# Stick-breaking values in a decoder layer: high and low part of a head's values side by side as one stationary block of 128 columns, the two halves of the result summed afterwards

## The reference, cut to what matters

```
def one_block(args):                      # 128 queries against all keys
    z = einsum('bhqd,bhkd->bhqk', q_blk, kf)
    log_beta = log_sigmoid(z)
    log_rem = where(mask, log_sigmoid(-z), 0.0)
    later = cumsum(log_rem, axis=3, reverse=True) - log_rem
    w = where(mask, exp(log_beta + later), 0.0)
    return einsum('bhqk,bhkd->bhqd', w, vf)
```

## Time and profile before

| | us |
|---|---|
| median of 3 runs (2136.02 to 2138.6) | 2136.45 |
| the profiled execution | 2141.96 |
| its span in the profile | 2140.1 |
| PE busy in the span | 2021.9 |
| stick-breaking stage, 600 to 880 us of the span | 280.0 |
| PE busy in that stage | 263.73 |

### The profile page before, as it was taken

One profiled execution on the slowest core, in us unless ns is written; L12 is line 12 of the kernel. 1 busy time (PEld: TensorE's weight loads), 2 busy tenths in 40 slices (PEclk: granted clock), 3 DMA queues, 4 the chain that ended last, 5 costly groups with the idle time before them and its releaser, 6 DMA issues. The chain is left out here.

```text
span 2140.1 us, 25998 instructions
## 1 busy us (share of the span) xinstructions
PE 2021.9 (94%) x10096; PEld 1663.2 (78%) x10096; DVE 990.7 (46%) x1106; ACT 706.2 (33%) x1083; POOL 988.4 (46%) x543
## 2 busy tenths in 40 slices
PE   7999999999999999998978998979999999999986
PEld 6888888788877777886858886857888888888866
DVE  5557475500056665325382224268445544411646
ACT  2323223301045555311152223054343333332344
POOL 4132232333434454445856452867455545544422
PEclk9999999999999999999979999999999999999998
DMA  5021120122100000311112110122222222354442
GB/s 181 30 86 43 57 78 29 49 78 69 69 21 21 21 30 21 119 41 48 39 60 79 59 59 21 38 106 92 89 74 84 79 89 79 120 204 138 131 159 94
DMA packets 54229, 159.76 MB, mean 75 GB/s; under 512 B 5632, under 2 KB 11904, under 8 KB 53120
## 3 DMA queue, kind: packets, MB, share of 16 engines
q1 hardware_dynamic: 47344, 134.47, 19.1%
q10 hardware_dynamic: 6800, 24.12, 3.0%
HBM read 134.45 MB, written 24.12 MB: 74 GB/s over the span
## 5 line engine op out<-in xcount | busy, mean ns | idle before, releaser
L483 POOL TENSOR_TENSOR w_hi<-w_raw,one 128x1024 fp32r<-128x1024 f32 x70 | 133.3, 1904 | 524.2 <-PE unit L667 524.2
L667 PE MATMUL unit<-x_lo,w_hi 128*128 128x512 f32 x752 | 295.0, 392 | 12.8 <-POOL w_lo L497 11.7
L671 PE MATMUL unit<-x_hi,w_hi 128*128 128x512 f32 x752 | 293.6, 390 | 0.0
L673 PE MATMUL unit<-x_hi,w_lo 128*128 128x512 f32 x752 | 293.6, 390 | 0.0
L486 POOL TENSOR_TENSOR w_lo<-w_raw,w_hi 128x1024 fp32r<-128x1024 f32 x70 | 173.9, 2485 | 5.5
L667 PEld LDWEIGHTS unit<-x_lo,w_hi 128*128 128x128 f32 x752 | 141.7, 188 | 43.9 <-POOL w_lo L497 11.7
L673 PEld LDWEIGHTS unit<-x_hi,w_lo 128*128 128x128 f32 x752 | 141.6, 188 | 29.8
L671 PEld LDWEIGHTS unit<-x_hi,w_hi 128*128 128x128 f32 x752 | 141.8, 189 | 29.3
L624 POOL TENSOR_TENSOR beta<-beta,stick 128x128 f32<-128x128 f32 (+7 forms) x64 | 77.1, 1205 | 150.4 <-DVE stick L1853 150.4
L1853 DVE TENSOR_TENSOR_SCAN stick<-stick 128x128 f32<-128x128 f32 (+7 forms) x64 | 106.3, 1662 | 49.8 <-ACT stick L1271 49.8
L667 PE MATMUL unit<-a_lo,w_hi 128*128 128x512 f32 x256 | 102.8, 401 | 9.7 <-DVE a_lo L1916 9.7
(11 more groups left out here) (518 smaller groups left out, 5533.5 us busy)
## 6 DMA issues: line engine op xcount, KB each, us to landing
w_raw<-stream SPq DMA_DIRECT2D x141, 512.0 KB, 3.5
w_next<-stream SPq DMA_DIRECT2D x34, 512.0 KB, 4.0
hidden_store<-hidden SPq DMA_DIRECT2D x22, 512.0 KB, 2.7
h_raw<-hidden_store SPq DMA_DIRECT2D x44, 256.0 KB, 3.8
rope_sb<-rope ACTq DMA_DIRECT2D x8, 1024.0 KB, 6.7
w_next<-stream SPq DMA_DIRECT2D x12, 384.0 KB, 3.3
acc<-xT ACTq DMA_DIRECT2D x8, 512.0 KB, 10.2
ret_branch<-acc ACTq DMA_DIRECT2D x8, 512.0 KB, 2.6
```

What stands on the lines that cost most here:

```text
L483: pool.tensor_tensor(w_hi[s][:, 0:width], w_raw[:, s, 0:width], one[:].to_broadcast([P, width]), ALU.mult).then_inc(w_hi_done, 1)
L667: x = pe.matmul(out, w_hi[s][:, wk], lo[:, k, cols], start=first, stop=False, skip_group_check=True)
L671: pe.matmul(out, w_hi[s][:, wk], hi[:, k, cols], start=False, stop=False, skip_group_check=True)
L673: last = pe.matmul(out, w_lo[s][:, wk], hi[:, k, cols], start=False, stop=(k == kts - 1), skip_group_check=True)
```

## The change

The value tiles `sv_hi` and `sv_lo` become one tile `sv`, in which each block of 128 keys has, per head, its 64 high columns and right behind them its 64 low columns. A matmul with this block of 128 columns as stationary operand gives the product with the high part in partitions 0 to 63 of the result and that with the low part in partitions 64 to 127. A head's value product is now N matmuls with `wT_hi`, behind a wait for `wt_hi`, and then N matmuls with `wT_lo`, behind the wait for `wt_split`. It has the term low·low in addition, which was left out before. ACT copies both halves out (four copies of 64x256 in place of two), the low one into a new tile `sb_low`, and DVE adds it to `sb_out` (`fold`, one instruction per two steps, at the end of the odd iterations).

```diff
 def sb_values(g, hd):
-    pe.wait_ge(wt_split, 2 * g + hd + 1)
+    pe.wait_ge(wt_hi, 2 * g + hd + 1)
...
         if g and qt % 2 == 0:
-            pe.wait_ge(sbo_stored, g)
+            pe.wait_ge(sbo_stored, 2 * g)
-    out = aux[0:SB_DIM, 2, c0:c0 + P]
+    out = aux[:, 2, c0:c0 + P]
     for b in range(qt + 1):
-        keys = slice(b * P, (b + 1) * P)
-        x = triple(out, sv_hi[p % 2][:, b, v], sv_lo[p % 2][:, b, v], wT_hi[:, hd, keys], wT_lo[:, hd, keys],
-                   b == 0, b == qt)
+        pe.matmul(out, sv[p % 2][:, b, hd, :, :].rearrange("p a d -> p (a d)"), wT_hi[:, hd, b * P:(b + 1) * P],
+                  start=b == 0, stop=False, skip_group_check=True)
+    pe.wait_ge(wt_split, 2 * g + hd + 1)
+    for b in range(qt + 1):
+        x = pe.matmul(out, sv[p % 2][:, b, hd, :, :].rearrange("p a d -> p (a d)"),
+                      wT_lo[:, hd, b * P:(b + 1) * P], start=False, stop=b == qt, skip_group_check=True)

 # ACT, at the end of an even iteration
     act.wait_ge(sbo_ready, g // 2)
+    if g > 4:
+        act.wait_ge(sb_folded, g // 2 - 2)
     for hd in range(2):
-        act.activation(sb_out[hd * SB_DIM:(hd + 1) * SB_DIM, pair, two * 2 * P:(two + 1) * 2 * P],
-                       aux[0:SB_DIM, 2, hd * 2 * P:(hd + 1) * 2 * P], ACT.Copy).then_inc(sbo_stored, 1)
+        rows, cols = slice(hd * SB_DIM, (hd + 1) * SB_DIM), slice(hd * 2 * P, (hd + 1) * 2 * P)
+        act.activation(sb_out[rows, pair, two * 2 * P:(two + 1) * 2 * P], aux[0:SB_DIM, 2, cols], ACT.Copy
+                       ).then_inc(sbo_stored, 1)
+        act.activation(sb_low[rows, (g // 2 - 1) % 2, :], aux[SB_DIM:P, 2, cols], ACT.Copy
+                       ).then_inc(sbo_stored, 1)

 # DVE
+def fold(e):
+    pair, two = divmod(e, QT // 2)
+    dve.wait_ge(sbo_stored, 4 * e + 4)
+    r = sb_out[:, pair, two * 2 * P:(two + 1) * 2 * P]
+    dve.tensor_tensor(r, r, sb_low[:, e % 2, :], ALU.add).then_inc(sb_folded, 1)
...
     if g < STEPS:
         scan(g, 1)
         if g in FILL_ENDS:
             drain_fill(FILL_ENDS[g])
+    if g > 1 and g % 2:
+        fold(g // 2 - 1)
+fold(STEPS // 2 - 1)
```

More of the change, by code:

```diff
@@ L109, in layer_program @@
         x_lo = sb(ctx, "x_lo", [P, KT, SEQ], F32R)
-        sq_hi, sq_lo, sk_hi, sk_lo, sv_hi, sv_lo, beta = [], [], [], [], [], [], []
+        sq_hi, sq_lo, sk_hi, sk_lo, sv, beta = [], [], [], [], [], []
         def stick_set(stack, j):
@@ L114, in stick_set @@
                 to.append(sb(stack, f"{name}{j}", [P, SEQ], F32R))
-            for to, name in ((sv_hi, "sv_hi"), (sv_lo, "sv_lo")):
-                to.append(sb(stack, f"{name}{j}", [P, QT, P], F32R))
+            sv.append(sb(stack, f"sv{j}", [P, QT, 2, 2, SB_DIM], F32R))
             beta.append(sb(stack, f"beta{j}", [P, 2, SEQ]))
@@ L172, in layer_program @@
                 vT = sb(s2, "vT", [P, SEQ])
-            for pieces in (sq_hi, sq_lo, sk_hi, sk_lo, sv_hi, sv_lo, beta):
+                sb_low = sb(s2, "sb_low", [P, 2, 2 * P])
+            for pieces in (sq_hi, sq_lo, sk_hi, sk_lo, sv, beta):
                 pieces.reverse()
@@ L263, in layer_program @@
             sem(n) for n in ("w_ready", "wt_ready", "wt_hi", "wt_split", "sbo_ready", "sbo_stored"))
+        sb_folded = sem("sb_folded")
         sbo_hi_done, sbo_split, branch_summed = sem("sbo_hi_done"), sem("sbo_split"), sem("branch_summed")
@@ L811, in sb_values @@
                     if g and qt % 2 == 0:
-                        pe.wait_ge(sbo_stored, g)
+                        pe.wait_ge(sbo_stored, 2 * g)
                 c0 = hd * 2 * P + qt % 2 * P
-                out = aux[0:SB_DIM, 2, c0:c0 + P]
-                v = slice(hd * SB_DIM, (hd + 1) * SB_DIM)
+                out = aux[:, 2, c0:c0 + P]
                 for b in range(qt + 1):
-                    keys = slice(b * P, (b + 1) * P)
-                    x = triple(out, sv_hi[p % 2][:, b, v], sv_lo[p % 2][:, b, v], wT_hi[:, hd, keys], wT_lo[:, hd, keys],
-                               b == 0, b == qt)
+                    pe.matmul(out, sv[p % 2][:, b, hd, :, :].rearrange("p a d -> p (a d)"), wT_hi[:, hd, b * P:(b + 1) * P],
[4 more added lines that the diff above has]
+                                  wT_lo[:, hd, b * P:(b + 1) * P], start=False, stop=b == qt, skip_group_check=True)
                 if qt % 2 and hd:
@@ L1264, in _ @@
             act.wait_ge(unit_ready, U_SB + 4)
-            act.activation(sv_hi[0][:].rearrange("p b d -> p (b d)"), unit[:, 1, :], ACT.Copy).then_inc(sv_hi_done, 1)
+            act.activation(sv[0][:, :, :, 0, :], unit[:, 1, :].rearrange("p (b h d) -> p b h d", h=2, d=SB_DIM), ACT.Copy
+                           ).then_inc(sv_hi_done, 1)
             def read_z(g, hd):
@@ L1305, in _ @@
                     act.wait_ge(v_turned, p)
-                    act.activation(sv_hi[p % 2][:], aux[:, 0:2, :].rearrange("p b (t d) -> p (b t) d", d=P), ACT.Copy
-                                   ).then_inc(sv_hi_done, 1)
+                    act.activation(sv[p % 2][:, :, :, 0, :], aux[:, 0:2, :].rearrange(
+                        "p b (t h d) -> p (b t) h d", h=2, d=SB_DIM), ACT.Copy).then_inc(sv_hi_done, 1)
                 if g < STEPS:
@@ L1314, in _ @@
                     act.wait_ge(sbo_ready, g // 2)
+                    if g > 4:
+                        act.wait_ge(sb_folded, g // 2 - 2)
                     for hd in range(2):
-                        act.activation(sb_out[hd * SB_DIM:(hd + 1) * SB_DIM, pair, two * 2 * P:(two + 1) * 2 * P],
-                                       aux[0:SB_DIM, 2, hd * 2 * P:(hd + 1) * 2 * P], ACT.Copy).then_inc(sbo_stored, 1)
-            act.wait_ge(sbo_stored, 8 * SB_PAIRS)
+                        rows, cols = slice(hd * SB_DIM, (hd + 1) * SB_DIM), slice(hd * 2 * P, (hd + 1) * 2 * P)
[3 more added lines that the diff above has]
+                                       ).then_inc(sbo_stored, 1)
+            act.wait_ge(sbo_stored, 16 * SB_PAIRS)
             for n in range(KT):
@@ L1322, in _ @@
             for k in range(4):
-                act.wait_ge(sbo_stored, 8 * SB_PAIRS)
+                act.wait_ge(sb_folded, 4 * k + 4)
                 act.activation(sbo_hi[:, k, :], sb_out[:, k, :], ACT.Copy).then_inc(sbo_hi_done, 1)
@@ L1839, in _ @@
             dve.wait_ge(sv_hi_done, 1)
-            dve.tensor_tensor(sv_lo[0][:].rearrange("p b d -> p (b d)"), unit[:, 1, :],
-                              f32(sv_hi[0][:].rearrange("p b d -> p (b d)")), ALU.subtract).then_inc(unit_drained[1], 1)
+            dve.tensor_tensor(sv[0][:, :, :, 1, :], unit[:, 1, :].rearrange("p (b h d) -> p b h d", h=2, d=SB_DIM),
+                              f32(sv[0][:, :, :, 0, :]), ALU.subtract).then_inc(unit_drained[1], 1)
             def mask_z(g):
@@ L1885, in _ @@
                     dve.wait_ge(sv_hi_done, p + 1)
-                    dve.tensor_tensor(sv_lo[p % 2][:], aux[:, 0:2, :].rearrange("p b (t d) -> p (b t) d", d=P),
-                                      f32(sv_hi[p % 2][:]), ALU.subtract).then_inc(sv_split, 1)
+                    dve.tensor_tensor(sv[p % 2][:, :, :, 1, :], aux[:, 0:2, :].rearrange(
+                        "p b (t h d) -> p (b t) h d", h=2, d=SB_DIM), f32(sv[p % 2][:, :, :, 0, :]), ALU.subtract
+                                      ).then_inc(sv_split, 1)
                 if g < STEPS:
```

## The result

| | before | changed |
|---|---|---|
| median, us | 2137.52 (4 runs) | 2152.93 (4 runs) |
| profiled execution / its span | 2141.96 / 2140.1 | 2152.57 / 2150.8 |

The changed kernel takes 1.0074 times the time of the one before (95% interval 1.0061 to 1.0086), some 15.5 us more. The two profiled spans differ by only 10.7 us, nearly the sum of the prediction, and this is misleading: the profiled execution before was 4.4 us over its median, and what follows the stage, where nothing was changed, took 1261.3 us in it (878.81 to 2140.1) against 1258.6 in the changed kernel's. Why is not settled: behind the stage the clock was at its 1.2 GHz level for some 70 us in both (69.4 and 70.4 us from 900 us on). The account has to be made inside the stage.

The account below looks back on a forecast made before the run. PE was taken to bound the stick-breaking stage (busy 263.73 of 280 us). Terms 9.3 - 1.9 - 0.5 + 2.3 + 0.4 + 0.9 = +10.5 us put the median at 2147 us, own range 2142 to 2153, 8 in 10 from 2138 to 2157.

Parts of the forecast that it names:

- The bound, the pace and its price: Value products on PE: 0.112 us per wide matmul against 0.060 narrow, set by the stationary load; +9.3 us.
- the helpers' +0.4: Iteration 3 of each pair: ACT's longer copies end the scan about 0.1 us later, four times; +0.4 us.
- 81 ns per matmul for 128 moving columns: Rival on the value products: a block costs 0.162 in place of 0.180 us, -5.2 us, 2132 us; chance 0.03.
- ACT's copies at the seams: At three pair seams, two more copies delay the chain to PE by 0.75 us each; +2.3 us.
- the 1.9 named as a sign: At the pair seams, turn_next_v would wait 1.9 us in place of 1.16 if the forecast is right.
- DVE's addition and the copies in iteration 3: Addition delays POOL's chain into iteration 11's wait, 3 x 0.3 = +0.9 us; copies in iteration 3, +0.4 us.
- The new wait order: Iteration 3 of each pair: high-pass matmuls run inside PE's wait for wT_lo; -0.48 us four times, -1.9 us.
- The step at the end: Last step: half clock until 876.1 us, matmuls done at 878.9 against 878.81; +0.1 where +0.6 was charged, so -0.5 us.
- The seams' half-clock stretches: Pair seams: a lower clock after the longer wait, 3 us at half level each, could add up to 4 us more.
- the helpers bind: Rival: longer ACT and DVE queues delay more than the seams, some +22 us, 2158 us; chance 0.13.
- the chain hides PE's time: Rival: the stage is bound by the chain, so PE's +9.3 us falls into 16.3 us idle time; 2137 us, chance 0.07.
- the load sets no limit: Rival: the 128 moving columns set 0.060 us per value matmul, -17.3 us, 2120 us; chance 0.04.

Follow-up runs that it names:

- the narrow run: Changed kernel with only the 64 high columns of sv as stationary operand in the same 2N matmuls, low part left out: 2135.75 us, ratio 0.9987.

## Why the prediction was right, and where it was not

**The bound, the pace and its price: right.** The value matmul costs 0.112 us, the distance of the loads, as in the rows from which the forecast took it, and the narrow operand takes 17 us and more away again. Where the clock was full, a seam costs 1.40 us more where 1.35 were forecast, a pair 1.62 where 1.66 (there two wrong parts, the helpers' +0.4 and the too large gain of the wait order, also cancelled). The Trainium skill, TensorE: Matmul & The Clock Gate, section Back-to-back issue gap, has 81 ns per matmul for 128 moving columns; this stream took 112 ns at full clock, and the measurement decides. The section LDWEIGHTS of the same page of the Trainium skill has columns / 1.2 ns; worked out as an estimate for 128 columns this is 107 ns, which is near.

**ACT's copies at the seams: right,** 0.8 us per seam taken away, 0.54 added alone, 0.75 forecast. But `turn_next_v` waits 1.64 us, not the 1.9 named as a sign: of the 0.8 us, 0.49 stand in this wait and 0.3 before the last transposes ahead of it (start 672.01), which the profile does not count as idle.

**DVE's addition and the copies in iteration 3: mis-sized, 1.3 us that did not come.** The kernel before with copies and addition lost only 2 us, 1.6 of them at the seams. In iteration 3 the scan swallowed the shift wholly: measured from the transposes of `vT` at the stage's start, it starts 0.9 us later than in the earlier trace rows and ends at the same time (24.2 us in both), since it overlaps POOL's split by 0.8 us in place of 1.7 and takes 1.89 in place of 2.80.

```profile
614.17 1.89 DVE L1862 TENSOR_TENSOR_SCAN stick<-stick 128x512 f32<-128x512 f32 x1 [1.15 <-ACT stick L1275]
```

The additions took 0.39 to 0.50 us where they met POOL's instructions for under 0.25 us, and up to 1.40 where they met them for 1.1; no wait of PE came of it. The Trainium skill, SBUF — State Buffer, section Who interferes with whom, says that such a DVE instruction contends with a GpSimd instruction that reads SBUF, and these times agree.

**The new wait order: the step failed, size 1 us.** "Behind the wait stood 0.70 us and now stand 0.45, four times" was credited in full. Two runs show that PE gets nothing of it between the seams: what the wait for `wT_lo` loses, the next transposes wait for `beta` or start later.

**The clock: the term that was mis-sized most.** The step at the end said "head 0's 16 matmuls do about 7 until 876.1 and the other 9 until 877.1": it took the moment when the clock comes back from the old trace, though the stream before that moment is what the change alters. +0.1 us was forecast, +1.6 came in the last step and +1.8 behind it. The seams' half-clock stretches (0.75 and 0.85 us in the profile) were named as a danger and not in the sum. These two make the 5 us between 10.5 and 15.5. That 2152.93 still lies in the sum's own range, 2142 to 2153, is luck: its upper 5 us were set aside for additions, which cost nothing, and the clock filled them. Two things in that range were also off: 512 intervals of 0.002 us are 1.0 us to each side, not 1.2, and its lower end follows from neither term.

**The rivals.** That the helpers bind is refuted by the run with their part alone; that the chain hides PE's time, by the stage's nearly unchanged idle time (though the narrow run shows the chain binding not far below); that the load sets no limit, by the loads' distance and the narrow run.

## What to carry to other kernels

Putting two narrow stationary operands side by side saved matmuls, not time, with a moving operand of 128 columns, as short as the stationary is wide: compare (count x load), read from a row of the same shape in the same trace. When a wait is shortened, follow its releaser's queue to the next wait of the same engine before crediting the gain. And where PE stands idle before a stretch that is changed, the clock's return belongs to the change as well; work moved into that idle time was the only thing here that made a kernel with the whole result faster.

## What the hardware showed that was not expected

With wide operands in the last step the clock stayed at the 1.2 GHz level for 10.2 to 13.7 us though PE had work without a gap (busy 5.00 of 5.00 us in the stretch above): a matmul every 0.2 us with 128 moving columns, and behind them 4 to 5 us of the gate projection. With 64-column operands in the same place it came back after 3.4 us. So here a gapless row of the profile did not tell when the clock would rise.
